# A two-layer decoder trunk: additions of the residual from VectorE to GpSimd for ten of sixteen row blocks

## The chip, the cores and the metric

The kernel runs on one core of a Trainium2 chip. A core has TensorE (matmuls), VectorE, ScalarE and GpSimd (elementwise work) and the DMA queues that SyncE issues. The metric is the device time in microseconds.

## The reference, cut to what matters

Two layers over x of 1024 positions by 1024 channels, in float32:

```python
for layer in range(DEPTH):
    mod = c_act @ mod_w[layer] + mod_b[layer]
    shift, scale, gate = jnp.split(mod, 3, axis=-1)
    h = rmsnorm(x, norm_g[layer]) * (1.0 + scale[:, None, :]) + shift[:, None, :]
    y = even_mixer(h, ...) if layer % 2 == 0 else odd_mixer(h, ...)   # both end in ... @ w_out
    x = x + gate[:, None, :] * y
return rmsnorm(x, final_g)
```

The mixers project h, mix along the positions and end in one output projection with 2048 input channels. What this case is about is the line `x = x + gate * y`.

## The kernel before

Each float32 product is made of three matmuls with operands split into an upper part, rounded by ScalarE (`w_hi`, L878, or L945 for y), and a lower part, the difference that VectorE makes (`w_lo`, L1407, or L1474 for y). Both VectorE instructions read two tensors in SBUF.

The output projection of a layer works on eight blocks of 128 rows of x, in passes: layer 0 has A (blocks 0, 1, 2), B (3, 4, 5) and C (6, 7), layer 1 has A (0 to 3) and B (4 to 7). A pass has 16 steps, one for each 128 input channels. In a step TensorE adds to every block of the pass, in two halves of 512 columns, each in its own PSUM bank; step n of pass B is called Bn here. The last two steps of a pass (three in the last one) are ordered by block, so that its halves become complete one after the other while the next pass starts.

A complete half is taken by VectorE in `residual` (L1847): a product of the bank with the gate's row into XN (L1857), then the sum of x's row block XR and XN into XR (L1861), which counts `o_evac` up. XR and XN are in SBUF. These things wait for `o_evac`:

- TensorE, in `free_bank` (L2261), before it starts a block of the next pass in that bank: in layer 0 for blocks 4, 5 and 7, in layer 1 for 4 to 7, where block 7 takes the banks of block 3.
- ScalarE, in `squares` (L1176): the sum of squares of a row block, its root, then, in layer 0, `normalize` (L1186) with the reciprocal that VectorE makes in `inverse` (L1864). The normalized rows of layer 0 are transposed by TensorE in three turns for layer 1's h.
- SP, in `rows_store` (L679), which sends a row block of layer 0 to DRAM; the loads of weights stand behind it in the same queue.

Every engine works through a list written out by hand. VectorE's and ScalarE's are in `passes`: residuals of blocks 0 and 1 come ahead of the splits of step B1, block 2 ahead of B2, block 3 and 4 ahead of C1 and the halves of block 5 ahead of C3 and C4; in layer 1 blocks 0 to 2 ahead of B1 and block 3 ahead of B2. The others (6, 7 and layer 1's 4 to 7) are taken when their pass is over. In layer 0 VectorE also adds rows of the modulation of layer 1 (L1843) after the splits of some steps. Column sums for this modulation run on TensorE in pass B (L2327).

Weights come through a ring of four raw slots. A load into a slot is issued when the lower half of what was in it is made. ScalarE's upper half waits for the load and for the slot of `w_hi` that TensorE frees.

GpSimd makes sums of weight blocks in `sums_of_weights` (L830) for the input projections of both layers. Between the last sum of layer 0 and the first one of layer 1, and behind the last of layer 1, its list is empty: that is where all output projections lie.

Of the kernel before, what the change touches and what calls it, by code (L numbers as in the profile page):

```python
# [7 lines left out]
ALU = mybir.AluOpType  # L8
# [20 lines left out]
WINDOWS = (2, 4, 8, 16)  # L29
GORDER = (0, 3, 2, 1)  # L30
PAD = max(WINDOWS)
DIRECT = KB - 1

S1, S2 = slice(0, HALF), slice(HALF, S)
HALVES = (S1, S2)
# [74 lines left out]
def build(nc, x, c, norm_g, mod_w, mod_b, hy_w_in, hy_conv_w, hy_conv_b, lru_w_a, lru_b_a, lru_w_x, lru_b_x,  # L110
# [102 lines left out]
    def raw_at(unit):  # L213
        return L[unit] % RAW

    def raw_landed(unit):
        return 16 * (L[unit] // RAW + 1)
# [13 lines left out]
    with ExitStack() as ctx:  # L231
        def sb(name, shape, dt=F32, stack=ctx):
            return stack.enter_context(nc.sbuf_tensor(name, shape, dt))

        def sem(name):
            return ctx.enter_context(nc.semaphore(name))
# [23 lines left out]
        rstd = sb("rstd", [P, 3, SB])  # L260
        pos = sb("pos", [P, PAD], mybir.dt.int32)
        icnt = sb("icnt", [P, GROUPS, PAD])
        fix = sb("fix", [P, PAD])

# [14 lines left out]
        with ExitStack() as phase:  # L279
            vps = [sb(f"vp{n}", [P, PAD + S], F32, phase) for n in range(2)]  # L280
            win = [sb(f"win{n}", [P, PAD + S], F32, phase) for n in range(2)]
            d_hi = sb("d_hi", [P, GB, S], F32R, phase)
# [13 lines left out]
        with ExitStack() as phase:  # L296
            sb("pad_pool", [P, 4, PAD + S], F32, phase)
            d_sums = sb("d_sums", [P, 2, GB, S], F32, phase)

        def flat(ap):  # L300
            return ap.rearrange("p a b -> p (a b)")
# [14 lines left out]
        def hx(k):  # L316

            return flat(whole_x[k // 2][:, 4 + k % 2, :, :])
# [14 lines left out]
        def stage(slot, kk):  # L333

            return stage_half(slot, kk // 4)[:, kk % 4, :]
# [7 lines left out]
        def t_sum(layer, kp, n):  # L343

            if n == 3:
                return halves(late[:, kp // 2, :] if layer == 0 else d_sums[:, 1, 2 + kp // 2, :])[:, kp % 2, :]
            if n == 2:
                return halves(aux[:, :] if layer == 0 else gb_[:, 2, :])[:, kp % 2, :]
            return halves(bufs[:, 8 + kp % 2, :] if layer == 0 else d_sums[:, 0, 2 + kp % 2, :])[:, n, :]
# [6 lines left out]
        def piece(at, width, dt=F32):  # L356
            if dt is F32R:
                return X.rearrange("p a b c d -> p (a b c d)")[:, at:at + width]
            kp, at = at // (14 * HALF), at % (14 * HALF)
            return whole_x[kp].rearrange("p a b c -> p (a b c)")[:, at:at + width]  # L360
# [11 lines left out]
        XR = ([bufs[:, (1, 6, 7, 9)[b % 4], :] for b in range(SB)], [piece(b * S, S) for b in range(SB)])  # L372
        XN = ([flat(whole_x[b % 4][:, 6, :, :]) for b in range(SB)], [piece((KB + b) * S, S) for b in range(SB)])
# [17 lines left out]
        xr_in = [sem(f"xr_in{n}") for n in range(4)]  # L391
# [73 lines left out]
        o_evac = sem("o_evac")  # L465
        part_made = sem("part_made")
# [30 lines left out]
        def full(name):  # L497

            if name[0] == "O" and name not in FULL:
                last = next(s for s in reversed(STEPS) if s[0] == name[1] and name[2] in BLOCKS[s[:2]])  # L500
                return o_step, Y[last] + 1
            return psum_full, FULL[name]

        def o_count(layer, b, half):

            return 2 * SB * layer + 2 * b + half + 1
# [310 lines left out]
        @block.gpsimd  # L817
        def _(pool):
            nc.gpsimd.memset(ident[:, :], 0.0).then_inc(const_step, 1)
            nc.gpsimd.memset(ones[:, :], 1.0).then_inc(const_step, 1)  # L820
            nc.gpsimd.memset(cst[:, 0:1], EPS).then_inc(const_step, 1)
            nc.gpsimd.memset(cst[:, 1:2], TINY).then_inc(const_step, 1)
            nc.gpsimd.iota(pos[:, :], [[1, PAD]], base=1, channel_multiplier=0).then_inc(const_step, 1)
            pool.wait_ge(const_step, 5)
            nc.gpsimd.affine_select(out=ident[:, :], in_=ident[:, :], compare_op=ALU.not_equal, fill=1.0, base=0,
                                    pattern=[[-1, P]], channel_multiplier=1).then_inc(const_step, 1)
            def raw_blocks(q, which):
                return raw[:, raw_at((("R1", "R2")[which], q)), :].rearrange("p (k two n) -> p two k n", two=2, n=P)

            def sums_of_weights(q):  # L830

                first, second = raw_at(("R1", q)), raw_at(("R2", q))
                even, odd = (ssum[:, n, :].rearrange("p (k n) -> p k n", k=KP) for n in range(2))
                a11, a12 = (raw_blocks(q, 0)[:, n, :, :] for n in range(2))
                a21, a22 = (raw_blocks(q, 1)[:, n, :, :] for n in range(2))
                pool.wait_ge(raw_in[second], raw_landed(("R2", q)))
                if q:
                    pool.wait_ge(lo_done, HI["p", q - 1, 4])
                nc.gpsimd.tensor_tensor(even, a21, a22, ALU.add).then_inc(s_ready, 1)  # L839
                pool.wait_ge(raw_in[first], raw_landed(("R1", q)))  # L840
                if q:
                    pool.wait_ge(lo_done, HI["p", q - 1, 5])
                pool.wait_ge(s_ready, 4 * q + 1)
                nc.gpsimd.tensor_tensor(odd, even, a11, ALU.add).then_inc(s_ready, 1)  # L844
                pool.wait_ge(lo_done, HI["p", q, 2])
                pool.wait_ge(s_ready, 4 * q + 2)
                nc.gpsimd.tensor_tensor(even, odd, a12, ALU.add).then_inc(s_ready, 1)  # L847
                pool.wait_ge(lo_done, HI["p", q, 3])
                pool.wait_ge(s_ready, 4 * q + 3)
                nc.gpsimd.tensor_tensor(odd, a21, a11, ALU.add).then_inc(s_ready, 1)  # L850

            def t1_and_t3(kp):

                if kp >= 2:
                    pool.wait_ge(t_lo, 3 * (kp - 1))
                pool.wait_ge(hhi_ready, 2 * kp + 2)
                even, odd = hx(2 * kp), hx(2 * kp + 1)
                nc.gpsimd.tensor_tensor(t_sum(0, kp, 0), even[:, S1], even[:, S2], ALU.subtract).then_inc(t13_added, 1)
                nc.gpsimd.tensor_tensor(t_sum(0, kp, 2), odd[:, S2], even[:, S2], ALU.subtract).then_inc(t13_added, 1)

            pool.wait_ge(*full(("ms", KB - 1)))
            for kp in range(KP):
                t1_and_t3(kp)
            for q in range(3 * (HEADS - 1)):
                sums_of_weights(q)

            for q in range(Q["V23", 0], len(PAIRS)):
                sums_of_weights(q)

        @block.scalar  # L870
        def _(act):
# [523 lines left out]
        def _(dve):  # L1395
# [117 lines left out]

            def accumulate(k, rows=range(DIRECT)):
                at, ring = k % 3, k % 2
# [229 lines left out]
            for i in range(1, HEADS):  # L1745
                a, b, cc = Q["A", i], Q["B", i], Q["C", i]
# [100 lines left out]
            def residual(layer, b, halves_=(0, 1)):  # L1847

                for half in halves_:
                    cols = HALVES[half]  # L1850
                    at = o_count(layer, b, half)
                    if (layer, half) == (0, 0) and b >= 4:
                        dve.wait_ge(*full(("T", b // 4 - 1 if b < 7 else 1, KB - 1)))
                    if (layer, b, half) == (1, 0, 0):
                        dve.wait_ge(gate_in, 32)
                    dve.wait_ge(*full(("O", layer, b, half)))
                    nc.vector.tensor_tensor(XN[layer][b][:, cols], area(("O", layer, b, half)),  # L1857
                                            (gate1 if layer else gate0)[:, cols], ALU.mult).then_inc(part_made, 1)
                    dve.wait_ge(part_made, at)
                    dve.wait_ge(xr_in[b % 4], 16 * (2 * layer + b // 4 + 1))  # L1860
                    nc.vector.tensor_tensor(XR[layer][b][:, cols], XR[layer][b][:, cols], XN[layer][b][:, cols],  # L1861
                                            ALU.add).then_inc(o_evac, 1)

            def inverse(layer, b):  # L1864
                at = SB * layer + b + 1
# [317 lines left out]
        def _(pe):  # L2183
# [187 lines left out]
            def mod_sums(k):  # L2371
# [3 lines left out]
                for part in range(2):  # L2375
                    nc.tensor.matmul(total[:, part:part + 1], stage(k % 3, DIRECT)[:, part * P:(part + 1) * P],
                                     ca[:, DIRECT:DIRECT + 1], start=part == 0, stop=False, skip_group_check=True)
                pe.wait_ge(macc_step, DIRECT * (k + 1))
                for part in range(2):
# [187 lines left out]
```

## Time and profile before

| | |
|---|---|
| median of 3 runs | 1310.0 us (1309.66 to 1310.04) |
| profiled execution, time | 1309.57 us |
| its span, first to last instruction | 1307.8 us |
| TensorE busy | 1275.5 us |
| VectorE busy | 936.9 us |
| ScalarE busy | 629.6 us |
| GpSimd busy | 273.2 us |
| mean granted clock of TensorE | 0.991 |

The profiled execution's time is 1.8 us more than its span, which is what lies around the instructions. Busy time is a share of the whole and says nothing of which wait ends last in a stretch. In a timeline a row is the start and the duration of an instruction in us; a bracket is the idle time of its engine before it and the instruction that ended it.

### The profile page before, as it was taken

What the parts mean: (1) busy time and instruction counts of PE and PEld (TensorE: products, weight loads), DVE (VectorE), ACT (ScalarE), POOL (GpSimd) and SP (SyncE); (2) the same over time, 40 slices, a digit from 0 to 9 for tenths busy, and PEclk for the clock granted to TensorE, in tenths of its full rate; (3) what the DMA queues carried; (4) which work ended last, traced back from release to release, by engine and by line L of the source; (5) the groups of instructions that cost most, each with busy time, mean ns of one, the idle gap of its engine ahead of it and who ended that gap; (6) DMA issues with size and microseconds to landing.
All of it is one profiled execution on the core that took longest, in us unless ns stands there. A gap on an engine that the chain in (4) does not pass through costs nothing.

```text
span 1307.8 us, 15401 instructions
## 1 busy us (share of the span) xinstructions
PE 1275.5 (98%) x5671; PEld 1051.3 (80%) x5671; DVE 936.9 (72%) x1123; ACT 629.6 (48%) x888; POOL 273.2 (21%) x158
## 2 busy tenths in 40 slices
PE   4999999999999999999999999999999999999997
PEld 3877888888888888887888788888888888888886
DVE  7889887878878887778477598758758656434636
ACT  6465656564646464545467474243243143222422
POOL 0034433433424332000000023133133131000000
PEclk8999999999999999999999999999999999999999
DMA  9712242323232341697748202320321321874441
GB/s 291 215 49 69 71 127 71 113 84 113 69 113 69 113 129 49 208 393 262 271 160 271 81 17 65 112 82 33 113 81 33 113 81 29 317 242 145 167 163 65
DMA packets 145618, 171.51 MB, mean 131 GB/s; under 512 B 6598, under 2 KB 117382, under 8 KB 145544
## 3 DMA queue, kind: packets, MB, share of 16 engines
q1 hardware_dynamic: 145544, 170.53, 40.4%
q8 instruction: 46, 0.75, 0.2%
q14 instruction: 28, 0.23, 0.1%
HBM read 145.33 MB, written 25.17 MB: 130 GB/s over the span
## 4 chain that ended last, share of the span: by engine, by line
PE 86%; DVE 8%; issue 2%; SPq 2%; ACT 1%; DMA 1%; DVEq 0%; ACTq 0%
PE psum L2186 28%; PE psum L2188 28%; PE psum L2187 28%; DVE whole_x L1857 1%; DVE w_lo L1407 1%; SPq L586 1%; DVE bufs L1640 1%; DVE X L1497 1%; DMA raw<-in_hy_w_out 1%; ACT w_hi L878 1%; PE psum L2321 0%; DVE w_lo L1429 0%; SPq L575 0%; DMA whole_x<-in_mod_w 0%; DVE late L1490 0%
## 5 line engine op out<-in xcount | busy, mean ns | idle before, releaser
L2186 PE MATMUL psum<-X,w_hi 128*128 128x512 f32 x1140 | 446.5, 392 | 2.5 <-DVE w_lo L1407 1.2
L2188 PE MATMUL psum<-X,w_lo 128*128 128x512 f32 x1140 | 444.6, 390 | 0.0
L2187 PE MATMUL psum<-X,w_hi 128*128 128x512 f32 x1140 | 444.6, 390 | 0.0
L2186 PEld LDWEIGHTS psum<-X,w_hi 128*128 128x128 f32 x1140 | 214.7, 188 | 49.7 <-issue 3.1
L2188 PEld LDWEIGHTS psum<-X,w_lo 128*128 128x128 f32 x1140 | 214.6, 188 | 44.8
L2187 PEld LDWEIGHTS psum<-X,w_hi 128*128 128x128 f32 x1140 | 214.6, 188 | 44.4 <-issue 0.2
L1407 DVE TENSOR_TENSOR w_lo<-raw,w_hi 128x1024 fp32r<-128x1024 f32 x98 | 120.4, 1231 | 159.3 <-ACT w_hi L878 159.1
L878 ACT ACTIVATE w_hi<-raw 128x1024 fp32r<-128x1024 f32 x98 | 103.6, 1057 | 201.9 <-PE psum L2188 162.8
L900 ACT ACTIVATE w_hi<-ssum 128x512 fp32r<-128x512 f32 x140 | 87.1, 626 | 120.8 <-PE psum L2188 91.1
L1429 DVE TENSOR_TENSOR w_lo<-ssum,w_hi 128x512 fp32r<-128x512 f32 x140 | 118.8, 856 | 23.8 <-ACT w_hi L900 23.2
L839 POOL TENSOR_TENSOR ssum<-raw 128x512 f32<-128x512 f32 x35 | 62.8, 1795 | 288.6 <-DMA raw<-in_pool_w_in 254.8
L847 POOL TENSOR_TENSOR ssum<-ssum,raw 128x512 f32<-128x512 f32 x35 | 55.8, 1595 | 310.0 <-DVE w_lo L1429 310.0
L2186 PE MATMUL psum<-w_hi,X 128*128 128x512 f32 x256 | 99.7, 389 | 0.3 <-DVE whole_x L1861 0.3
L2188 PE MATMUL psum<-w_hi,X 128*128 128x512 f32 x256 | 99.6, 389 | 0.0
L2187 PE MATMUL psum<-w_lo,X 128*128 128x512 f32 x256 | 99.6, 389 | 0.0
L850 POOL TENSOR_TENSOR ssum<-raw 128x512 f32<-128x512 f32 x35 | 78.5, 2243 | 79.2 <-DVE w_lo L1429 79.2
L844 POOL TENSOR_TENSOR ssum<-ssum,raw 128x512 f32<-128x512 f32 x35 | 62.1, 1774 | 48.2 <-DVE w_lo L1429 46.2
L1421 DVE TENSOR_TENSOR w_lo<-raw,w_hi 128x1024 fp32r<-128x1024 f32 x35 | 42.7, 1220 | 25.6 <-ACT w_hi L889 25.4
L2186 PEld LDWEIGHTS psum<-w_hi,X 128*128 128x128 f32 x256 | 48.0, 188 | 10.6 <-DVE whole_x L1861 0.7
L2188 PEld LDWEIGHTS psum<-w_hi,X 128*128 128x128 f32 x256 | 48.0, 188 | 10.0
L2187 PEld LDWEIGHTS psum<-w_lo,X 128*128 128x128 f32 x256 | 48.1, 188 | 9.9
L2186 PE MATMUL psum<-d_hi,w_hi 128*128 128x512 f32 x128 | 49.9, 390 | 0.3 <-DVE w_lo L1407 0.3
(244 smaller groups left out, 1946.1 us busy)
## 6 DMA issues: line engine op xcount, KB each, us to landing
raw<-in_hy_w_in SPq DMA_DIRECT2D x48, 512.0 KB, 5.1
raw<-in_hy_w_out SPq DMA_DIRECT2D x48, 512.0 KB, 5.1
raw<-in_pool_w_in SPq DMA_DIRECT2D x32, 512.0 KB, 4.9
raw<-in_pool_w_out SPq DMA_DIRECT2D x32, 512.0 KB, 3.8
aux<-in_mod_w SPq DMA_DIRECT2D x16, 512.0 KB, 4.2
y_dram<-bufs SPq DMA_DIRECT2D x16, 512.0 KB, 3.1
raw<-in_mod_w SPq DMA_DIRECT2D x16, 512.0 KB, 5.6
y_dram<-gb_ SPq DMA_DIRECT2D x16, 512.0 KB, 3.2
```

What stands on the lines that cost most here:

```text
L839: nc.gpsimd.tensor_tensor(even, a21, a22, ALU.add).then_inc(s_ready, 1)
L844: nc.gpsimd.tensor_tensor(odd, even, a11, ALU.add).then_inc(s_ready, 1)
L847: nc.gpsimd.tensor_tensor(even, odd, a12, ALU.add).then_inc(s_ready, 1)
L850: nc.gpsimd.tensor_tensor(odd, a21, a11, ALU.add).then_inc(s_ready, 1)
L878: nc.scalar.activation(flat(w_hi[:, es:es + 2, :]), raw[:, at, :], ACT.Copy).then_inc(hi_done, 1)
L900: nc.scalar.activation(w_hi[:, es, :], ssum[:, op % 2, :], ACT.Copy).then_inc(hi_done, 1)
L1407: nc.vector.tensor_tensor(flat(w_lo[:, es:es + 2, :]), raw[:, at, :], flat(w_hi[:, es:es + 2, :]).bitcast(F32), ALU.subtract).then_inc(lo_ ...
L1421: ins = nc.vector.tensor_tensor(w_lo[:, es:es + 2, :].rearrange("p two (k n) -> p two k n", k=KP), raw_blocks(q, 0), w_hi[:, es:es + 2, :] ...
L1429: ins = nc.vector.tensor_tensor(w_lo[:, es, :], ssum[:, op % 2, :], w_hi[:, es, :].bitcast(F32), ALU.subtract)
L2186: nc.tensor.matmul(out_, whi, xhi, start=first, stop=False, skip_group_check=check)
L2187: nc.tensor.matmul(out_, whi, xlo, start=False, stop=False, skip_group_check=check)
L2188: return nc.tensor.matmul(out_, wlo, xhi, start=False, stop=last, skip_group_check=check)
```

## The change

The additions of blocks 0 to 5 of layer 0 and 0 to 3 of layer 1 are made by GpSimd, half by half. The products stay on VectorE. GpSimd waits for the product (`part_made`) and for the load of x's rows. Its additions of layer 0 stand in its list behind the last sum of weights of layer 0, those of layer 1 at its end. Where VectorE makes the additions that follow (blocks 6 and block 4 of layer 1), it first waits until all before have been counted.

```diff
+ADDED_ON_POOL = [(0, b) for b in range(6)] + [(1, b) for b in range(4)]
...
             for q in range(3 * (HEADS - 1)):
                 sums_of_weights(q)
+            def residual(layer, b):
+
+                for half, cols in enumerate(HALVES):
+                    at = o_count(layer, b, half)
+                    pool.wait_ge(part_made, at)
+                    pool.wait_ge(xr_in[b % 4], 64 if layer else 16 * (b // 4 + 1))
+                    nc.gpsimd.tensor_tensor(XR[layer][b][:, cols], XR[layer][b][:, cols], XN[layer][b][:, cols],
+                                            ALU.add).then_inc(o_evac, 1)
+
+            for b in range(6):
+                residual(0, b)
 
             for q in range(Q["V23", 0], len(PAIRS)):
                 sums_of_weights(q)
+            for b in range(4):
+                residual(1, b)
...
                     nc.vector.tensor_tensor(XN[layer][b][:, cols], area(("O", layer, b, half)),
                                             (gate1 if layer else gate0)[:, cols], ALU.mult).then_inc(part_made, 1)
-                    dve.wait_ge(part_made, at)
-                    dve.wait_ge(xr_in[b % 4], 16 * (2 * layer + b // 4 + 1))
-                    nc.vector.tensor_tensor(XR[layer][b][:, cols], XR[layer][b][:, cols], XN[layer][b][:, cols],
-                                            ALU.add).then_inc(o_evac, 1)
+                    if (layer, b) not in ADDED_ON_POOL:
+                        dve.wait_ge(part_made, at)
+                        dve.wait_ge(xr_in[b % 4], 16 * (2 * layer + b // 4 + 1))
+                        if b == 6 or (layer, b) == (1, 4):
+                            dve.wait_ge(o_evac, at - 1)
+                        nc.vector.tensor_tensor(XR[layer][b][:, cols], XR[layer][b][:, cols], XN[layer][b][:, cols],
+                                                ALU.add).then_inc(o_evac, 1)
```

## Rows read from the trace of the kernel before

**Rows 1.** The page: busy time and share of each engine.
```profile
PE 1275.5 (98%) x5671; PEld 1051.3 (80%) x5671; DVE 936.9 (72%) x1123; ACT 629.6 (48%) x888; POOL 273.2 (21%) x158
```

**Rows 2.** Timeline of TensorE's instructions with idle time, in three stretches.
```profile
608.01 0.47 PE L2186 MATMUL psum<-w_hi,y_at_r 128*128 128x512 f32 x1 [0.26 <-DVE y_at_r L1474]
620.77 0.47 PE L2186 MATMUL psum<-w_hi,y_at_r 128*128 128x512 f32 x1 [0.27 <-DVE y_at_r L1474]
...
677.02 0.47 PE L2186 MATMUL psum<-w_hi,y_at_r 128*128 128x512 f32 x1 [0.22 <-DVE y_at_r L1474]
685.52 0.19 PEld L2186 LDWEIGHTS psum<-w_hi,y_at_r 128*128 128x128 f32 x1 [0.49 <-DVE w_lo L1407]
...
1217.35 0.50 PE L2186 MATMUL psum<-w_hi,X 128*128 128x512 f32 x1 [0.27 <-DVE whole_x L1861]
```

**Rows 3.** Timeline of VectorE and ScalarE, layer 0, turn from A to B.
```profile
596.14 0.69 DVE L1861 TENSOR_TENSOR bufs<-bufs,whole_x 128x512 f32<-128x512 f32 x1
596.75 0.68 DVE L1857 TENSOR_TENSOR whole_x<-psum,late 128x512 f32<-128x512 f32 x1
...
599.00 1.06 ACT L878 ACTIVATE w_hi<-raw 128x1024 fp32r<-128x1024 f32 x1 [6.01 <-PE psum L2188]
...
600.73 1.22 DVE L1407 TENSOR_TENSOR w_lo<-raw,w_hi 128x1024 fp32r<-128x1024 f32 x1
...
603.53 0.68 DVE L1857 TENSOR_TENSOR whole_x<-psum,late 128x512 f32<-128x512 f32 x1
...
606.18 1.22 DVE L1407 TENSOR_TENSOR w_lo<-raw,w_hi 128x1024 fp32r<-128x1024 f32 x1
...
607.31 0.55 DVE L1474 TENSOR_TENSOR y_at_r<-bufs,y_at_r 128x384 fp32r<-128x384 f32 x1
```

**Rows 4.** Timeline of GpSimd, two sums that follow each other.
```profile
67.39 1.30 POOL L859 TENSOR_TENSOR aux<-whole_x 128x512 f32<-128x512 f32 x1
68.64 1.30 POOL L858 TENSOR_TENSOR bufs<-whole_x 128x512 f32<-128x512 f32 x1
```

**Rows 5.** Timeline of VectorE and GpSimd, where their work overlaps in layer 0.
```profile
208.82 0.68 DVE L1429 TENSOR_TENSOR w_lo<-ssum,w_hi 128x512 fp32r<-128x512 f32 x1
...
209.59 1.30 POOL L847 TENSOR_TENSOR ssum<-ssum,raw 128x512 f32<-128x512 f32 x1 [9.70 <-DVE w_lo L1429]
209.62 0.69 DVE L1458 TENSOR_TENSOR bufs<-bufs,psum 128x512 f32<-128x512 f32 x1
...
217.70 1.28 DVE L1664 SCALAR_TENSOR_TENSOR bufs<-bufs,vec 128x1022 f32<-128x1022 f32 x1
...
217.93 2.20 POOL L839 TENSOR_TENSOR ssum<-raw 128x512 f32<-128x512 f32 x1 [4.14 <-DVE w_lo L1429]
...
218.89 1.79 DVE L1429 TENSOR_TENSOR w_lo<-ssum,w_hi 128x512 fp32r<-128x512 f32 x1
```

**Rows 6.** Timeline of VectorE and ScalarE, layer 0, turn from B to C.
```profile
668.70 0.68 DVE L1857 TENSOR_TENSOR whole_x<-psum,late 128x512 f32<-128x512 f32 x1
...
671.47 1.06 ACT L1180 ACTIVATE whole_x<-bufs 128x1024 f32<-128x1024 f32 x1 [3.33 <-DVE bufs L1861]
...
678.73 0.68 DVE L1857 TENSOR_TENSOR whole_x<-psum,late 128x512 f32<-128x512 f32 x1
...
681.72 1.16 ACT L1188 ACTIVATE whole_x<-bufs,rstd 128x1024 f32<-128x1024 f32 x1 [2.26 <-DVE rstd L1867]
...
682.78 1.04 ACT L878 ACTIVATE w_hi<-raw 128x1024 fp32r<-128x1024 f32 x1
```

**Rows 7.** Timeline of VectorE, layer 1, turn from A to B: block 3.
```profile
1214.55 0.68 DVE L1857 TENSOR_TENSOR whole_x<-psum,whole_x 128x512 f32<-128x512 f32 x1
...
1216.60 0.69 DVE L1861 TENSOR_TENSOR whole_x<-whole_x 128x512 f32<-128x512 f32 x1
```

**Rows 8.** Busy time by stretch; last: granted clock, DMA share, GB/s.
```profile
628.80:632.30 3.50, 3.50 (x10) 2.73 (x9) 2.24 (x5) 1.62 (x3) 0.00 (x0) 0.51 0.97 377
```

**Rows 9.** The chain that ended last, a piece of it in that stretch.
```profile
630.20 0.43 PE psum L2187
```

## The prediction

> **What bounds the kernel now.** I read the page first: TensorE is busy for 1275.5 of the 1307.8 us [rows 1], so work taken from VectorE shortens the run only where TensorE stands waiting for VectorE, and work made later lengthens it wherever TensorE or its feeders wait for that work. Then I listed every TensorE instruction with idle time in front of it in the three stretches where the additions are made: the turn from pass A to B of layer 0 (590 to 625 us), from B to C (665 to 700) and from A to B of layer 1 (1200 to 1220). There are five [rows 2]: the first four wait for VectorE's split of the weights or of y, the last, 1217.35, for an addition itself (L1861). Idle time and the slower first matmul make some 0.4 us each, so everything that these waits could give back is about 2 us, and the tail behind 1288 us isn't touched, since blocks 4 to 7 of layer 1 stay on VectorE. Last I read the timelines of VectorE, ScalarE and GpSimd in those stretches, to lay the new order over the old.
>
> **What is removed and what is added.** Twenty additions (ten blocks, two halves) of 0.69 us leave VectorE (the row of L1861) [rows 3]: 13.8 us of busy time, but only the shift of what is behind them counts. The same twenty run on GpSimd. The trace has no addition of these tiles there; the nearest are GpSimd's sums of two 128x512 SBUF operands, 1.30 us alone, and 1.26 from start to start when two follow each other [rows 4]. They begin some 0.1 us after VectorE's releasing instruction: L1429 ends at 209.50, GpSimd starts at 209.59 [rows 5]. So an addition that used to end 0.7 us behind its product now ends about 1.4 behind it. Bounds: 1.30 from below, and 2.2, as in the row at 217.93, where it meets VectorE. The VectorE waits on o_evac ahead of blocks 6 and of (1, 4) cost nothing: GpSimd has finished by then and the engine waits for its own last addition anyway; at worst 0.1 us each.
>
> **The collision.** Rows 5 show what matters most. At 209.59 GpSimd adds in 1.30 us while VectorE runs an addition with a PSUM operand in 0.69: neither is longer than alone. At 217.93 GpSimd is released while VectorE runs L1664, which reads two SBUF operands and ends at 218.98; GpSimd takes 2.20, that is 0.9 us of waiting and 1.3 of work, and ends at 220.13. VectorE's L1429, also with two SBUF operands, is issued at 218.89 and takes 1.79 where 0.68 is usual: it stands still until GpSimd is done. So a GpSimd addition and a VectorE instruction with two SBUF operands never run together, and they alternate. The products with the gate (one operand in PSUM) are free of this, but the splits L1407 and L1474, which TensorE waits for, are not. By the two ends of those rows an addition keeps VectorE out for 1.79 - 0.68 = 1.1 us. The Trainium skill ("SBUF — State Buffer", section "Who interferes with whom") says that such a pair excludes each other for the whole instruction, whoever issues first. By that, with the full 1.30 for each, the three places below would come to 0.2 us more each, about 4.3 us instead of 3.7; I keep to the row's 1.1.
>
> **Layer 0, A to B** [rows 3]. Before: a product, its addition at 596.14, the next product 0.61 behind that, and so on for four halves; the split of step B1 starts at 600.73, the products of block 2 at 603.53, the split of B2 at 606.18, its y at 607.31, and TensorE goes on at 608.01. After: the first product still ends at 596.1, the other three follow at 0.61 each and end at 598.0; the additions run from 596.2 to 601.3. The split of B1 can't use the room: ScalarE makes its upper half only by 600.06 (L878 at 599.00). It comes just as the fourth addition starts, waits until 601.2 and ends at 602.3 (before 601.95). What stands between it and the products of block 2 is 0.4 late with it, so these begin at 603.9 and end at 605.2. Its first addition has the read path from 604.7 to 606.0, the split of B2 follows until 607.1, then the second addition until 608.3, and only then y, done at 608.8 (before 607.86). TensorE goes on at 608.95: +0.95 us. That alternation takes what the two missing additions gave (1.4 us) and 0.9 more. What follows (the split of B3, the release of raw's slot, the next load, the wait at 620.77) is the same chain shifted by 0.95 with TensorE, and TensorE waits for nothing between 621 and 676 [rows 2], so it stays. Bounds of this term: 0 (the lock tie at 600.1 and the later one fall for VectorE) to 1.3.
>
> **Layer 0, B to C** [rows 6]. ScalarE's square of block 3 has waited 3.33 us for the second addition, at 671.47, and behind it in ScalarE's queue stand normalize, the upper half for C1, then VectorE's split and TensorE at 677.02. From the product at 668.70: second product ends 670.0, first addition 669.5 to 670.8, second to 672.05. +0.6 us for the whole chain, with no collision, as VectorE has only products and a reciprocal there. Then block 5's first product, at 678.73 before, comes at 679.35; VectorE issues the split of C3 at 680.0, ahead of GpSimd, and keeps it to 681.1; GpSimd's addition takes to 682.3; y waits for it and ends at 682.65; the reciprocal of block 4 behind it, which ScalarE waits for at 681.72 before, comes 1.1 later; the upper half of C4 (682.78 before), its split and TensorE at 685.52 follow: +1.1 in all, the 0.6 included. SP's stores of blocks 3 and 5 wait for the additions, and the loads of weights behind them start 0.6 to 1.8 us later. Before the turns that follow there is over 1 us between a split and its use, so I count nothing; that is the weakest of the zeros, up to +0.7 if one lands late. Bounds of the term: 0.6 to 1.8.
>
> **Layer 1, A to B** [rows 7]. Blocks 0 to 2 are no matter: six additions from about 1205 at 1.26 end near 1213, and TensorE wants those banks from 1212 on, in their order. Block 3 is what TensorE waits for: its bank is given free by the addition, not by the product. Before: product 1214.55, addition, product, addition from 1216.60 to 1217.29, TensorE at 1217.35. After: products at 1214.55 and 1215.16; first addition 1215.4 to 1216.7; the split of the next weights, two SBUF operands, is issued at 1215.8 and runs 1216.6 to 1217.75; the second addition, kept out by it, 1217.75 to 1218.95; TensorE at 1219.0: +1.65 us. Without the split's turn it would be 1217.95, +0.6. Bounds 0.6 and 1.9. TensorE is the bound from there to 1288, so nothing is given back.
>
> **Sum.** 0.95 + 1.1 + 1.65 = 3.7 us. Against the profiled execution (span 1307.8, time 1309.57) this is 1313.3; that execution is 0.4 below the median of the runs, so by the median 1313.7 us, +0.28%. 0.2% (2.6 us) is about what a measurement of this kernel can tell from no change.
>
> **The rivals.** (a) *The engines don't hinder each other on these tiles.* Then VectorE is 2 us ahead at B2 and the waits at 608.01 and 620.77 go (-0.8), the square of block 3 still costs 0.6, of which 0.3 is left at 685.52, and layer 1 costs 0.6: +0.1, 1310.1 us (0.8, then 0.3 and 0.6). For it: VectorE's relief is real, and ties may fall well. Against it: the 1.79 us of 218.89. It decides if L1407 behind 605 us takes 1.2 us beside a running addition. This is the case that isn't slower. (b) *The slow stretch of TensorE goes.* From 628.8 to 632.3 the granted clock is 0.51, which is 1.2 of 2.4 GHz, behind the column sums of the modulation [rows 8]; a matmul takes 0.43 us of the chain there [rows 9], which at the upper level would be 0.2 less, 1.6 us for some eight of the ten in it. The sums now come 0.95 later; if the clock doesn't fall behind them, the total is 3.7 - 1.6 = 2.1, 1312.1 us. Against it: the sums themselves are the same. (c) *It falls once more*, behind the longer wait in layer 1, or a late load adds its 0.7: 3.7 + 0.7 to 3.7 + 1.6 + 0.7, 1314.4 to 1316, with 1315.5 as its time. Against the clock: no row of before shows a fall behind two waits of about 1 us. (d) *VectorE's relief counts elsewhere*: 13.8 us of busy time less would make the kernel faster only where TensorE waits for it, at most the 2 us of the five rows, 1308.0 us, and 1306.4 with the 1.6 of (b). Against it: three of the five get longer by the steps above.
>
> **How the numbers follow.** Forecast 0.66, its own range 1312.8 to 1314.8 (the terms between 0.5, 0.9, 1.4 and 1.2, 1.5, 1.8, with the execution's scatter); (a) 0.14, (b) 0.06, (c) 0.11, (d) 0.03. Slower: 0.66 less 0.05 for the smallest terms, and (c): 0.72. Faster: (d), 0.03. Same: (a), (b) and the 0.05, 0.25. The range from 1310.6 to 1316.0 leaves out (d), most of (a) and the end of (c).
>
> **What would show it.** In the changed profile: twenty GpSimd instructions on whole_x and bufs, 1.3 us alone and up to 2.4 where they wait; L1857 in rows 0.62 apart; L1474 near 607 and 681, or L1407 near 606 and 1216, over 0.5 us longer than before; TensorE's waits behind 608 and 1217 grown to about 1.2 and 2 us, the last one with GpSimd as its releaser; the square of block 3 0.6 later. Wrong would be: L1407 and L1474 at their old durations (then a), a missing half-clock stretch behind 629 us (b), a second one or a late load (c).

## The result, and the profile after

The changed kernel takes 1315.43 us (median of 7 runs, 1310.96 to 1315.8) against 1309.66 us before (7 runs, 1309.1 to 1310.22). The medians are 5.8 us apart (0.44%); the ratio estimated from all the runs is 1.0036, 95% interval 1.0026 to 1.0045. It is slower, by a few tenths of a per cent. The profiled execution took 1315.76 us, its span is 1314.0, 6.2 more than before.

First the TensorE instructions with idle time at the three turns, which answer to [rows 2] (line numbers have moved: L2204 is the old L2186, L1422 and L1489 are the splits L1407 and L1474, L1872 the product, L874 GpSimd's addition, L893 ScalarE's upper half, L1195 its square):

```profile
608.27 0.47 PE L2204 MATMUL psum<-w_hi,y_at_r 128*128 128x512 f32 x1 [0.99 <-DVE y_at_r L1489]
621.37 0.47 PE L2204 MATMUL psum<-w_hi,y_at_r 128*128 128x512 f32 x1 [0.57 <-DVE y_at_r L1489]
...
679.74 0.47 PE L2204 MATMUL psum<-w_hi,y_at_r 128*128 128x512 f32 x1 [0.79 <-DVE y_at_r L1489]
688.65 0.47 PE L2204 MATMUL psum<-w_hi,y_at_r 128*128 128x512 f32 x1 [0.46 <-DVE y_at_r L1489]
...
1221.33 0.50 PE L2204 MATMUL psum<-w_hi,X 128*128 128x512 f32 x1 [0.28 <-POOL whole_x L874]
1223.53 0.51 PE L2204 MATMUL psum<-w_hi,X 128*128 128x512 f32 x1 [1.24 <-POOL whole_x L874]
```

All five waits of before are still there, longer. The first was 0.26 and is 0.99; the one at 677.02 was 0.22 and is 0.79; the one at 1217.35, in front of the second half of block 3's bank, was 0.27 and is the 1.24 at 1223.53. Layer 1 also has a new one, 0.28 at 1221.33, in front of the first half. The releaser of both is now GpSimd.

The timeline of VectorE, GpSimd and ScalarE, merged where instructions of a kind follow each other (x4 is four of them), at the turn from A to B of layer 0, then B to C, then layer 1, answers to [rows 3, 6, 7]:

```profile
594.96 2.48 DVE L1872 TENSOR_TENSOR whole_x<-psum,late 128x512 f32<-128x512 f32 x4
595.72 5.05 POOL L874 TENSOR_TENSOR bufs<-bufs,whole_x 128x512 f32<-128x512 f32 x4 [81.11 <-DVE whole_x L1872]
599.63 2.22 DVE L1422 TENSOR_TENSOR w_lo<-raw,w_hi 128x1024 fp32r<-128x1024 f32 x1 [2.20 <-ACT w_hi L893]
...
604.20 3.51 POOL L874 TENSOR_TENSOR bufs<-bufs,whole_x 128x512 f32<-128x512 f32 x2 [3.42 <-DVE whole_x L1872]
604.64 1.92 DVE L1422 TENSOR_TENSOR w_lo<-raw,w_hi 128x1024 fp32r<-128x1024 f32 x1
...
606.49 1.64 DVE L1489 TENSOR_TENSOR y_at_r<-bufs,y_at_r 128x384 fp32r<-128x384 f32 x1
...
674.19 1.06 ACT L1195 ACTIVATE whole_x<-bufs 128x1024 f32<-128x1024 f32 x1 [3.89 <-POOL bufs L874]
...
682.06 1.21 DVE L1422 TENSOR_TENSOR w_lo<-raw,w_hi 128x1024 fp32r<-128x1024 f32 x1
682.22 2.20 POOL L874 TENSOR_TENSOR bufs<-bufs,whole_x 128x512 f32<-128x512 f32 x1 [4.39 <-DVE whole_x L1872]
683.19 1.51 DVE L1489 TENSOR_TENSOR y_at_gbp<-bufs,y_at_gbp 128x256 fp32r<-128x256 f32 x1
...
1219.99 3.49 POOL L874 TENSOR_TENSOR whole_x<-whole_x 128x512 f32<-128x512 f32 x2 [2.66 <-DVE whole_x L1872]
1220.42 1.93 DVE L1422 TENSOR_TENSOR w_lo<-raw,w_hi 128x1024 fp32r<-128x1024 f32 x1
1222.28 1.75 DVE L1489 TENSOR_TENSOR X<-whole_x,X 128x512 fp32r<-128x512 f32 x1
```

Read durations, not starts. Four additions between which no two-operand instruction of VectorE runs take 5.05 us, 1.26 each. The pair at 604.20 takes 3.51 instead of 2.5, since a split stands between the two; that split takes 1.92 instead of 1.22 and the split of y behind it 1.64 instead of 0.55. At 682 the same in the other order: L1422 is first and undisturbed at 1.21, GpSimd takes 2.20, and L1489 waits for it, 1.51 instead of 0.42. The first split, at 599.63, has to wait for the fourth addition and loses 1.0 us (2.22 instead of 1.22).

Then the clock. Busy time by stretch (last columns: granted clock, DMA share, GB/s), which answers to [rows 8], and a piece of the chain, the column sums and a matmul behind them:

```profile
627.70:634.50 6.80, 6.80 (x24) 5.93 (x24) 3.50 (x6) 1.99 (x3) 0.00 (x0) 0.50 1.00 348
740.30:743.80 3.50, 3.50 (x9) 2.73 (x10) 2.11 (x4) 2.10 (x5) 1.57 (x2) 0.51 0.85 227
```

```profile
625.70 4.68 PE psum L2345 x32
...
631.44 0.43 PE psum L2206
```

Before there was one such stretch in the middle of the kernel, from 628.8 to 632.3, and the column sums took 3.46 us, all of them at the full clock; the same 32 now take 4.68, since the clock falls while they run. A third stretch, behind 740, is new in kind: it follows the two waits of TensorE at the start of layer 1's projections, which are 0.82 and 1.20 us in this profile and 0.83 and 1.21 before.

To part these two, I compared the starts of the same TensorE matmul in both traces. The 5671 matmuls come in the same order in every kernel here but the last one of the table, where 28 places between 625 and 634 us differ. So the difference of two starts is what a kernel has lost up to there:

```
start of the same matmul, kernel minus before, us; the column is the time before
                        607    612   622.5   660    690    730   744.5  1200   1216   1280
the change            -0.46   0.30   0.57   2.16   3.11   3.08   4.65   4.67   5.11   6.19
the change, again     -0.51   0.22   0.21   1.81   2.75   2.73   2.73   2.73   3.16   5.87
blocks 0-2 alone      -0.85  -0.09  -0.56   1.01   1.01   0.95   0.94   0.91   0.91   0.90
blocks 3-5 alone       0.09   0.13   0.18   0.17   1.14   1.10   1.12   1.10   1.10   1.11
layer 1 alone          0.12   0.12  -0.06  -0.07  -0.04  -0.07  -0.09  -0.08   0.36   1.44
banks by product       0.34   1.07   1.09   1.07   2.00   2.00   3.56   3.58   3.57   2.99
split waits            0.76   1.52   1.81   3.42   4.35   4.35   4.34   4.34   4.77   4.88
delay only            -0.19   0.95   0.42   0.43   0.46   0.43   2.06   2.07   2.07   2.08
reordered             -0.80  -1.31  -1.86  -1.87  -2.53  -2.58  -2.56  -2.59  -2.59  -3.17
reordered, changed    -0.53  -1.04  -1.57  -1.58  -1.49  -0.05   1.57   1.59   1.58   1.00
same, store later     -1.11  -1.62  -1.78  -1.82  -1.79  -1.84  -1.84  -1.85  -1.86  -2.44
reordered, pieces     -0.91  -1.42  -1.97  -3.60  -4.29  -4.35  -2.83  -2.81  -2.82  -3.40
```

In the first column nothing of the change has run yet: what stands there is how the two executions differ anyhow. For the change itself: 1.03 us up to 622.5, 0.95 from 660 to 690, 1.52 from 1200 to 1280, in sum 3.5 us at the three turns. The rest, 1.59 between 622.5 and 660 and 1.57 at 744.5, lies where the clock rows are. So 3.5 us of the change's own waits and 3.2 us of lower clock, less the 0.5 of the start, make the 6.2.

### The profile page after: what moved, and what is told of

It is laid out like the page before. It is cut to its first block, busy times and chain, and to the rows that moved or that the text cites. A ratio compares the mean times of both kernels' runs of the same rounds, so it can differ in the third digit from the quotient of the medians.

```text
span 1314.0 us, 15401 instructions
## 1 busy us (share of the span) xinstructions
PE 1278.9 (97%) x5671; PEld 1054.3 (80%) x5671; DVE 929.5 (71%) x1103; ACT 629.3 (48%) x888; POOL 301.3 (23%) x178
## 4 chain that ended last, share of the span: by engine, by line
PE 81%; DVE 8%; issue 6%; SPq 2%; DMA 1%; ACT 1%; POOL 0%; POOLq 0%; DVEq 0%; ACTq 0%
PE psum L2204 27%; PE psum L2205 26%; PE psum L2206 26%; DVE w_lo L1422 1%; SPq L588 1%; DVE whole_x L1872 1%; ACT w_hi L893 1%; DVE bufs L1655 1%; DVE X L1512 1%; DMA raw<-in_hy_w_out 1%; PE psum L2339 0%; DVE w_lo L1444 0%; SPq L577 0%; DMA whole_x<-in_mod_w 0%; DMA whole_x<-x_dram 0%
## 5 line engine op out<-in xcount | busy, mean ns | idle before, releaser
L2204 PE MATMUL psum<-X,w_hi 128*128 128x512 f32 x1140 | 447.0, 392 | 2.5 <-DVE w_lo L1422 1.2
L2204 PEld LDWEIGHTS psum<-X,w_hi 128*128 128x128 f32 x1140 | 214.8, 188 | 49.8 <-issue 3.1
L1422 DVE TENSOR_TENSOR w_lo<-raw,w_hi 128x1024 fp32r<-128x1024 f32 x98 | 122.8, 1254 | 167.7 <-ACT w_hi L893 167.2
L893 ACT ACTIVATE w_hi<-raw 128x1024 fp32r<-128x1024 f32 x98 | 103.6, 1057 | 206.1 <-PE psum L2206 163.5
L2204 PE MATMUL psum<-w_hi,X 128*128 128x512 f32 x256 | 99.8, 390 | 1.5 <-POOL whole_x L874 1.5
L2204 PEld LDWEIGHTS psum<-w_hi,X 128*128 128x128 f32 x256 | 48.0, 188 | 12.2 <-POOL whole_x L874 2.4
L874 POOL TENSOR_TENSOR bufs<-bufs,whole_x 128x512 f32<-128x512 f32 x12 | 17.1, 1453 | 155.0 <-DVE whole_x L1872 155.0
```

Of the source, the lines that this page charges most:

```text
L893: nc.scalar.activation(flat(w_hi[:, es:es + 2, :]), raw[:, at, :], ACT.Copy).then_inc(hi_done, 1)
L1422: nc.vector.tensor_tensor(flat(w_lo[:, es:es + 2, :]), raw[:, at, :], flat(w_hi[:, es:es + 2, :]).bitcast(F32), ALU.subtract).then_inc(lo_ ...
L2204: nc.tensor.matmul(out_, whi, xhi, start=first, stop=False, skip_group_check=check)
```

## The experiments

Each kernel ran beside the kernel before on its chip. The median of the kernel before was 1309.96 us (31 runs) beside the three turns and the banks by the product; 1309.67 (29) beside the split that waits, the delay, the other order and the change once more; 1309.74 (18) beside the change on the other order and the sums in pieces; 1309.46 (13) beside the later store. Every table column and every wait below is from one profiled execution of a kernel; the medians are over all its runs.

**The three turns one at a time.** The list of blocks is cut; a GpSimd addition that follows one of VectorE's waits for it.

```diff
-ADDED_ON_POOL = [(0, b) for b in range(6)] + [(1, b) for b in range(4)]
+ADDED_ON_POOL = [(0, b) for b in range(3)]       # first kernel
+ADDED_ON_POOL = [(0, b) for b in range(3, 6)]    # second
+ADDED_ON_POOL = [(1, b) for b in range(4)]       # third
```

Expected of the first: 

> Only blocks 0 to 2 of layer 0 are added on GpSimd. Theory: GpSimd's additions and VectorE's splits exclude each other; TensorE's waits at the turn from A to B grow by 1.0 us in sum (1.06 in the profile of the change), the waits at the turn to C and in layer 1 are as before. Time: +1.0 us over the kernel before, and +1.6 or +3.2 more in runs in which a stretch at the lower TensorE clock is added. Rival: the loss is spread over the kernel by something else, such as the slower clock alone; then this third of the change shows about no wait of its own. Rival of the lone slower engine: without exclusion the split of y for B2 ends at or before its old time and the turn costs nothing or gains up to 0.8.

Measured: 1312.12 us (1310.62 to 1313.0), ratio 1.0014 (1.0004 to 1.0023). Its waits at the turn:

```profile
607.91 0.47 PE L2208 MATMUL psum<-w_hi,y_at_r 128*128 128x512 f32 x1 [1.01 <-DVE y_at_r L1493]
```

This is the 0.99 of the change again, while the wait that used to follow near 620.8 is gone. In the table the turn costs 0.76 at B2 and gives 0.47 back at B5, so 0.3 and not 1.0. The wait at B5 ends with a load of weights; over the profiles with GpSimd additions there it moved this second part between -0.5 and +0.3. The profile also has 1.57 us of clock between 622.5 and 660, so 1.9 of the 2.2 us between the medians is accounted for. The expectation was right on place and clock, and wrong on the second wait.

Expected of the second: 

> Only blocks 3 to 5 of layer 0 are added on GpSimd. Theory: the square of block 3 comes 0.6 us later since an addition ends 0.7 later on GpSimd, and the split of y for C3 is kept out by 1.1 us; TensorE's waits at the turn from B to C grow by 0.9 to 1.1 us, the other turns are as before. Time +1.0 us, in steps of 1.6 more where the clock falls once more. Rival without exclusion: +0.3.

Measured: 1311.86 us (1310.63 to 1313.75), 1.0018 (1.0009 to 1.0028); in the table +0.97 from 660 to 690, and nothing elsewhere, as expected. The medians are 1.9 us apart, more than that; the four executions at 1311.05 us and below, the profiled one among them, have a mean granted clock of 0.990 or 0.991, the six above them 0.989, so lower clock is the likely rest.

Expected of the third: 

> Only blocks 0 to 3 of layer 1 are added on GpSimd. Theory: TensorE waits twice for block 3's banks, +1.5 us over before, nothing at layer 0's turns; time +1.5 us, and with no shift in layer 0 the stretches at the lower clock are those of before. Rival without exclusion: +0.6.

Measured: 1311.3 us (1310.33 to 1312.61), 1.0012 (1.0003 to 1.0022); +1.52 from 1200 to 1280:

```profile
1216.58 0.50 PE L2208 MATMUL psum<-w_hi,X 128*128 128x512 f32 x1 [0.28 <-POOL whole_x L876]
1218.78 0.51 PE L2208 MATMUL psum<-w_hi,X 128*128 128x512 f32 x1 [1.24 <-POOL whole_x L876]
```

The parts at B2, from B to C and in layer 1 have the size that they have in the whole change; only the second wait at B5 doesn't. So the loss isn't spread over the kernel.

**TensorE waits for the product.** The bank is read by the product only, so it can be reused before the addition.

```diff
-                    pe.wait_ge(o_evac, o_count(0, b - 4 if b < 6 else 3, half))
+                    pe.wait_ge(part_made, o_count(0, b - 4 if b < 6 else 3, half))
...
-                    pe.wait_ge(o_evac, o_count(1, b - 4, half))
+                    pe.wait_ge(part_made, o_count(1, b - 4, half))
```

> The change, with TensorE's waits for a free bank of the next pass on the product (part_made) and no longer on the addition (o_evac); the bank is read by the product alone. Theory: both waits of TensorE behind block 3 of layer 1 are gone (1.9 us of them against the change, so 0.4 less than before there); layer 0's turns keep their +2.0, since there TensorE waits for splits. Time about 1.9 us under the change in runs with the same stretches of the lower clock, +1.6 over before. Rival: the loss in layer 1 is in the splits kept out by the additions, and TensorE waits as long for y of B2 instead.

Measured: 1311.86 us (1308.52 to 1312.88), 1.0011 (1.0002 to 1.0021). In its profile TensorE has no wait between 1200 and 1230, and the table has -0.59 there where the change has +1.52, 2.1 us less (1.9 expected); nor does TensorE wait for y instead, as the rival said. Its splits behind block 3 take 1.94 and 1.78 us, as long as in the change, and nobody waits: a collision costs only where its victim is next on the path.

**The split waits for GpSimd.** In layer 1 VectorE starts the split for B2 only when both additions of block 3 are made.

```diff
                             if at == 2:
                                 residual(1, 3)
+                                dve.wait_ge(o_evac, o_count(1, 3, 1))
```

> The change, with one wait more on VectorE in layer 1: the split of the weights for B2 starts only when GpSimd has made the second addition of block 3. Theory (GpSimd and a VectorE instruction with two SBUF operands exclude each other): the second addition is no longer kept out, takes 1.3 us and not 2.2, and TensorE's second wait in layer 1 (1.24 us of idle time) shrinks by 0.9; the splits come later but 5 us ahead of use. Time 0.9 us under the change. Rival (GpSimd is only slow, nobody is kept out): the addition and TensorE's wait stay as they are.

Measured: 1312.5 us (1309.82 to 1314.55), 1.0020 (1.0011 to 1.0030). GpSimd, VectorE and TensorE there:

```profile
1219.66 2.52 POOL L874 TENSOR_TENSOR whole_x<-whole_x 128x512 f32<-128x512 f32 x2 [2.66 <-DVE whole_x L1872]
1222.21 1.23 DVE L1422 TENSOR_TENSOR w_lo<-raw,w_hi 128x1024 fp32r<-128x1024 f32 x1 [2.03 <-POOL whole_x L874]
...
1222.23 0.50 PE L2205 MATMUL psum<-w_hi,X 128*128 128x512 f32 x1 [0.27 <-POOL whole_x L874]
```

A wait more makes it faster. The pair of additions takes 2.52 us instead of 3.49, the split 1.23 instead of 1.93, TensorE's second wait is 0.27 instead of 1.24: 0.97 less, where 0.9 was expected. A GpSimd that is only slow would show none of it. The medians of this kernel and of the change beside it (1314.96) differ by more, 2.5 us; the table has one fall of the clock less in this profile, 1.6 us.

**A delay without GpSimd.** The kernel before, and one VectorE instruction (its result is used by nobody) ahead of the splits of B2:

```diff
                             if at == 2:
                                 residual(0, 2)
+                                nc.vector.tensor_tensor(bufs[:, 2, :], bufs[:, 5, :], bufs[:, 5, :], ALU.max)
```

> The kernel before, nothing on GpSimd, with one VectorE instruction of 128x1024 (about 1.2 us, SBUF to SBUF, its result is used by nobody) ahead of the splits of B2 in layer 0. Theory on the clock: the additional stretches at the lower clock come from when TensorE is delayed, not from GpSimd's work; so this kernel, with a delay of TensorE like that of additions for blocks 0 to 2 alone (about 1 us), shows the same two adjoining stretches at the column sums in part of its executions, and a time like that kernel's, about 2 us over before, of which 1.1 is the delay. Rival: the clock falls for GpSimd's sake; then +1.1 us and the single stretch of before.

Measured: 1310.93 us (1309.61 to 1312.81), 1.0010 (1.0001 to 1.0019). TensorE's wait at B2 and the clock by stretch:

```profile
608.96 0.47 PE L2187 MATMUL psum<-w_hi,y_at_r 128*128 128x512 f32 x1 [1.40 <-DVE y_at_r L1474]
```

```profile
629.00:632.40 3.40, 3.40 (x10) 2.63 (x10) 2.29 (x4) 1.56 (x3) 0.00 (x0) 0.51 1.02 366
738.20:741.60 3.40, 3.40 (x10) 2.62 (x9) 1.92 (x3) 1.56 (x4) 1.92 (x2) 0.50 0.68 188
```

GpSimd has nothing to do at these turns here, and the profile still shows the new stretch behind 738, 1.6 us in the table. At the column sums it has the single stretch of before, not the two that I had expected to be possible. Its ten times lie in two groups, five from 1309.61 to 1310.19 and five from 1311.66 up. The median is 1.3 us over before, and not 2: the delay costs 1.14 us at B2 and gives 0.53 back at B5. So a fall behind 738 comes without GpSimd's additions. The long stretch at the sums isn't settled by it: of the five profiles in the old order with blocks 0 to 2 on GpSimd four have it, and none of the seven others with the sums in one piece does, this one included. What the twelve profiles show is where the fall lies. In the four with the long stretch it comes while the column sums still run, and these take 3.85 to 4.70 us from the first of them to the matmul behind them; in the other eight it comes at most 0.2 us before their end, or behind it, and they take 3.48 to 3.55. The kernel before, too, has single times up to 1311.87 among these 29. What decides where the clock falls stays open.

**Another order, no GpSimd.** The banks by the product as above, and in VectorE's list block 2 behind the splits of B3, block 3 behind those of C0 and the reciprocal of block 4 ahead of block 5:

```diff
-                            if at == 2:
-                                residual(0, 2)
...
-                                residual(0, 3)
                                 residual(0, 4, (0,))
...
+                            if at == 3:
+                                inverse(0, 4)
                             if at in (3, 4):
                                 residual(0, 5, (at - 3,))
...
                         step_splits(y_step)
+                        if (layer, p, at) == (0, "B", 3):
+                            residual(0, 2)
+                        if (layer, p, at) == (0, "C", 0):
+                            residual(0, 3)
...
-                        if p == "C" and at in (3, 5):
-                            inverse(0, 4 if at == 3 else 5)
+                        if (p, at) == ("C", 5):
+                            inverse(0, 5)
```

> No addition on GpSimd: the kernel before in another order. TensorE waits for the product and not the addition before it reuses a bank; block 2 is taken behind the splits of B3, block 3 behind those of C0, and the reciprocal of block 4 ahead of block 5. Theory: TensorE's five waits at the three turns come from VectorE's order, so all five go, 2 us in sum, and the time is 2 us under before apart from the clock's stretches. Rival: the waits move to the next step of the same chain (the loads of weights), and less than 1 us is gained.

Measured: 1306.82 us (1305.71 to 1309.41), ratio 0.9978 (0.9969 to 0.9987), faster than both kernels. The totals of who waited for whom (us, times, longest), TensorE from 580 to 760 us (L1188 is `normalize`):

```profile
PE psum L2189 <- DVE w_lo L1407: 1.2, 1, 1.2
PE psum L2324 <- ACT whole_x L1188: 0.8, 1, 0.8
```

Only the two waits at the start of layer 1's projections are left; all five at the turns are gone, 2.4 us in the table (from -0.80 to -3.17), 2.9 between the medians; 2 was expected, and the rival's less than 1 is out.

**The change on the other order.** Both diffs together.

> The other order of the run before (banks freed by the product, block 2 behind the splits of B3, block 3 behind those of C0, the reciprocal of block 4 early) and the change on top: additions of the ten blocks on GpSimd. Theory: the additions still hold VectorE's splits up, by some 1 us at B1 and at C3, but the new order has put about as much room ahead of them, so TensorE waits for little: 0 to 0.5 us over the reordered kernel without the change, 1.5 to 2 under the kernel before. Rival: the collisions cost what they cost in the change (2 us in layer 0); then it is as slow as before.

Measured: 1309.54 us (1307.47 to 1311.83), 1.0000 (0.9991 to 1.0008): a miss, it gives the whole gain back. The rival's time came out, but not by its cause: TensorE has no wait at the turn from A to B, and two at the next one. TensorE and ScalarE:

```profile
675.87 0.47 PE L2207 MATMUL psum<-w_hi,y_at_r 128*128 128x512 f32 x1 [0.63 <-DVE y_at_r L1489]
...
688.88 1.06 ACT L893 ACTIVATE w_hi<-raw 128x1024 fp32r<-128x1024 f32 x1 [2.68 <-DMA raw<-in_hy_w_out]
...
691.68 0.47 PE L2207 MATMUL psum<-w_hi,y_at_gbp 128*128 128x512 f32 x1 [1.23 <-DVE y_at_gbp L1489]
```

At 675.87 it is the later square of block 3, which puts TensorE 0.73 us behind the reordered kernel without the change (the table's columns lie too far apart to show it alone); at 691.68 a load of weights, 1.44 in the table. SP's queue, first where it issues the store of block 5 (L681, L683) and the load behind it (L599, L601) without the change, then with it:

```profile
680.84 0.32 SPq L681 DMA_DIRECT2D x_dram<-bufs  x1
681.21 0.43 SPq L599 DMA_DIRECT2D raw<-in_hy_w_out  x1
```

```profile
683.21 0.32 SPq L683 DMA_DIRECT2D x_dram<-bufs  x1
683.58 0.43 SPq L601 DMA_DIRECT2D raw<-in_hy_w_out  x1
```

The store waits for the addition and the load stands behind the store: 2.4 us later than without the change, where TensorE is 1.0 us later. The profile with the change also has the clock stretch behind 737, 1.6.

**The store later.** The same kernel, with the store of block 5 behind the loads of C8.

```diff
-                if p == "C" and at in (3, 4, 5):
+                if p == "C" and at in (3, 4):
                     rows_store(at)
                 if (p, at) == ("C", 8):
+                    rows_store(5)
                     rows_load(0, 7)
```

> The reordered kernel with the change on top, and on SP the store of block 5's rows moved from behind the loads of C5 to behind those of C8, so that no load of weights stands behind the wait for block 5's addition. Theory: the 1.2 us of TensorE at 691.7 came from a load that SP issued 2.4 us late behind this store; it goes, and TensorE keeps only the 0.6 us at the start of C1 (the square of block 3). Time 1.2 to 1.4 us under the kernel without the move, some 1.3 over the reordered kernel without the change. Rival: the load is late for its slot or for the traffic on the DMA engines; then the wait stays.

Measured: 1307.73 us (1306.72 to 1309.74), 0.9984 (0.9974 to 0.9993), 1.8 under the run above (1.2 to 1.4 expected; that run's profile had one fall of the clock more). The wait at 691.68 is gone, and this is the only one of more than 0.2 us left at the turns:

```profile
675.60 0.47 PE L2208 MATMUL psum<-w_hi,y_at_r 128*128 128x512 f32 x1 [0.63 <-DVE y_at_r L1490]
```

So in the better order, too, the change gains nothing: this kernel is 0.9 us over the reordered one without it by the medians (1.3 expected), 1.0 in the table.

**The column sums in pieces.** The reordered kernel without the change, and the column sums (16 columns, 32 matmuls) in six pieces of 3, 3, 3, 3, 2 and 2 columns between the parts of step B6. Of the diff this is the place of the pieces; the sums in one piece behind B5 are left out, and what they waited for is waited for ahead of the first piece.

```diff
                             part_of(y_step, b, half)
+                            if (layer, p, n) == (0, "B", 6):
+                                piece_of_sums(2 * (b - 3) + half)
```

> The reordered kernel without the change, and the 32 column sums of the modulation (3.5 us of one-column matmuls in one piece behind B5) laid in six pieces between the parts of step B6. The work on TensorE is the same. Theory on the clock: the stretch at the lower level near 628 us follows this long piece; in pieces between wide matmuls it doesn't come, and the kernel is 1.6 us faster than the reordered one, about 1305.3. Rival: the clock falls all the same, since the sums lie in the same few us; then no change.

Measured: 1305.75 us (1304.49 to 1307.66), 0.9970 (0.9959 to 0.9980), the lowest median here. Clock by stretch:

```profile
623.50:630.90 7.40, 7.40 (x51) 6.72 (x50) 3.45 (x5) 3.29 (x5) 0.00 (x0) 1.00 0.74 275
732.70:736.10 3.40, 3.26 (x8) 2.62 (x9) 2.20 (x4) 2.25 (x6) 1.26 (x1) 0.50 0.95 247
```

The fall at the sums is gone, 1.6 us between 622.5 and 660 in the table, and this profile has one behind 732.7 instead, behind the same two waits as in the other kernels, which the reordered kernel's profile doesn't have. By the medians 1.1 us of the 1.6 stay, but the intervals of the two kernels' ratios overlap and they ran on different chips, so that gain in time isn't shown. That the fall at the sums is gone rests on this one profile against twelve; the pieces also spread the sums over the 7 us of B6, and cutting and spreading weren't parted.

**The change once more.**

> The changed kernel once more, for a second profile and more times. Theory: TensorE's waits at the turns are those of the first profile to 0.1 us, 3.5 us over before, while the stretches at the lower clock vary between executions from one to three in the middle of the kernel, so its times lie in groups 1.6 us apart, from about 1311 to 1316. Rival: the stretches are a fixed consequence of the change and every execution has the three.

Measured: 1314.96 us (1311.78 to 1316.11, 6 runs), 1.0036 (1.0025 to 1.0047). Clock by stretch:

```profile
628.20:635.00 6.80, 6.80 (x20) 5.54 (x20) 2.75 (x6) 1.99 (x3) 0.00 (x0) 0.50 0.99 365
1222.20:1225.60 3.40, 3.40 (x10) 2.63 (x9) 1.63 (x2) 2.69 (x5) 0.00 (x0) 0.50 0.00 0
```

TensorE's waits are those of the first profile but for the one at 621, which is 0.28 instead of 0.57. The clock falls at the column sums again, not behind 740, but right behind the long wait in layer 1. The same wait of 1.24 us has no fall behind it in the first profile and in that of layer 1 alone. So the falls change between executions of one program. The times of the 13 runs go with that: those of 1315.3 us and more have a mean granted clock of 0.988 to 0.990, the one of 1310.96 us has 0.994.

## Why the prediction was right, and where it wasn't

The forecast was 1313.7 us (+0.28%), 1310.6 to 1316.0, slower with 0.72; measured 1315.43 us, +0.44% by the medians and +0.36% by the ratio. Slower was right, and so were the waits that it was added up from. The time lies outside the forecast's own 1312.8 to 1314.8 and inside the whole range only because that took in rival (c), held at 0.11: that it fits so closely is in part luck. Of the 13 runs two lie in the forecast's own range, eight at 1315.3 and above, three below.

- **The collision** is right, order and price. The alternation of an addition, the split of the weights, an addition and the split of y came as laid out for 604.7 to 608.8, half a microsecond earlier by the execution's own start. VectorE was kept out by 1.0, 0.7 and 1.1 us. Of the two prices weighed there, 4.3 us with the whole 1.30 for each turn and 3.7 with 1.1, the lower one was nearer to the measured 3.5. The two exclude each other for the whole instruction: the split at 604.64 takes 1.92 us, and the pair of additions in layer 1 3.49, against 2.52 in the run in which the split waits, with nothing else changed. That agrees with what the Trainium skill ("SBUF — State Buffer", section "Who interferes with whom") says.
- **Layer 0, A to B**: 0.95 forecast, 0.76 at B2 and 1.03 with the wait at B5. That B5's wait would only move with the chain, at the same size, was wrong as a rule: it is 0.57, 0.28 or none in the profiles with additions there. The chain to it isn't simply shifted: its load of weights was issued at 614.68 before and at 614.25 in the change, and ScalarE took it up 3.15 us later before (617.83) and 4.19 later in the change (618.44). The five profiles with blocks 0 to 2 on GpSimd in this order give 0.3 to 1.05 for the turn.
- **Layer 0, B to C**: 1.1 forecast (0.6 and 0.5), measured 0.57 and 0.38.
- **Layer 1**: 1.65 forecast, 1.52 measured; without the split's turn 0.6 forecast, 0.55 in the run in which the split waits (from 4.34 to 4.88).
- **The sum**: 3.7 forecast, 3.5 measured in the profile. The text on (d) counts three of the five waits as growing; by the prediction's own steps it is four, and in the profile all five grew.
- **The clock** is what the profile has beside the waits, 3.2 us in two further stretches, and so what took the median from 1313.7 to 1315.4. It was held at "falls as before" in the forecast, with (c), one more fall, at 0.11 and 1315.5 us. The step that failed is the sentence against (c): "no row of before shows a fall behind two waits of about 1 us". In five profiles the clock fell behind just these two waits, which hadn't grown (the change, the banks by the product, the delay alone, the reordered kernel with the change and the sums in pieces). My place for it, the long wait in layer 1, was right in one profile of two; the others fell at the column sums, for twice the time, and behind 740.
- **The zero for late loads** from B to C held in the change and not in general: with the other order the same store made a load late and cost 1.4 us.

## What to carry to other kernels

Before you move work to an idle engine, look at which resources its instructions share and with whom: here GpSimd's additions cost 1.26 us each in which VectorE's two-operand instructions stand still, and what VectorE gained by 0.69 us each was worth nothing where TensorE waited for the split behind it. If TensorE waits for VectorE, look first at the order of VectorE's list and at which instruction the wait is really for: banks by the product and three moves gave 2.9 us by the medians (2.4 in the profile) with no work moved at all, and the change on top of them took 0.9 us or more of it back. And follow each consumer of a result that comes later through its whole queue, the SP's stores too.

## What the runs showed of the hardware that I had not expected

- TensorE's granted clock fell to the lower level (0.50 to 0.51 in the rows) at places that differ between executions of one program: in twelve profiles at or behind the 3.5 us of one-column matmuls, and not in the one in which these were laid in pieces between wide ones; in five of the thirteen behind the two waits of 0.8 and 1.2 us at the start of layer 1's projections; once behind 1.24 us of waiting in layer 1. Where it fell while the one-column matmuls still ran, the stretch was 6.8 us long and not 3.4 (four profiles of twelve). Each further 3.4 us at the lower level cost 1.5 to 1.6 us. The first seven times of the kernel before lie within 1.1 us (31 later ones within 3.0), those of the changed one within 4.8.
- GpSimd and VectorE take turns: in the rows shown, where both had two-operand work ready, one instruction of each went at a time (addition, split, addition, split of y from 604.20 on).
